# A mixture-of-experts block on one core: wider gathers of an expert's rows, and a search cut in three parts

## The reference

```python
g_prob = softmax(x @ w_rg + b_rg)            # 4 groups, the best one is taken
e_in_group = take_along_axis(e_logits, g_idx)  # 8 experts in it
e_top, e_idx = top_k(softmax(e_in_group), 2)   # the best two
expert = g_idx * 8 + e_idx                     # of 32 experts
...
def expert_block(args):
    xs, e = args
    gate, up = split(xs @ w_e_in[e], 2)        # 1024 x 1024 float32
    return (silu(gate) * up) @ w_e_out[e]      # 512 x 1024 float32
...
y = zeros((NT, D)).at[slot_tok].add(yb * slot_w[:, None])
x = x + gt2 * y
```

## Time and profile before

| | us |
|---|---|
| median of three runs | 1807.15 (1803.92 to 1807.35) |
| the profiled execution | 1807.53 |
| its span | 1805.7 |
| PE busy | 1682.9 (93% of the span) |
| DVE busy | 1014.3 (56%) |
| ACT busy | 442.2 (24%) |
| POOL busy | 235.0 (13%) |
| bytes moved | 334.20 MB, mean 185 GB/s |

### The profile page before, as it was taken

How to read it: one execution, slowest core, us unless ns; L and a number is a source line. 1 busy time by engine, 2 the same in 40 slices (tenths; PEclk the granted TensorE clock), 3 DMA queues, 4 the chain that set the end, 5 groups by cost and what they waited for, 6 DMA issues and landing times.

```text
span 1805.7 us, 35644 instructions
## 1 busy us (share of the span) xinstructions
PE 1682.9 (93%) x14825; PEld 932.5 (52%) x14825; DVE 1014.3 (56%) x2446; ACT 442.2 (24%) x1072; POOL 235.0 (13%) x359
## 2 busy tenths in 40 slices
PE   5999999999999999999999999969999998989890
PEld 3455444544445554555545545546777555555550
DVE  2486526564565345444444435556777777676754
ACT  5121323334443222222212311012222121212110
POOL 3030000000111122220222230010000000000003
PEclk9999999999999999999999999979999999999995
DMA  9377200001112011010110472368999999999997
GB/s 345 118 265 247 67 24 24 24 24 47 47 47 79 19 33 33 16 33 19 33 33 15 177 288 101 129 207 321 378 399 400 393 396 386 396 392 395 390 367 297
DMA packets 105413, 334.20 MB, mean 185 GB/s; under 512 B 13594, under 2 KB 57544, under 8 KB 93036
## 3 DMA queue, kind: packets, MB, share of 16 engines
q1 hardware_dynamic: 86256, 282.70, 42.2%
q0 software_dynamic: 8240, 25.04, 4.1%
q10 hardware_dynamic: 10828, 25.24, 3.9%
HBM read 299.51 MB, written 37.63 MB: 187 GB/s over the span
## 4 chain that ended last, share of the span: by engine, by line
PE 79%; DMA 14%; DVE 3%; issue 1%; POOL 1%; ACT 1%; SPq 1%; ACTq 0%; POOLq 0%; DVEq 0%
PE bank L296 77%; DMA arena<-in_w_e_in 10%; DMA arena<-in_w_e_out 2%; DMA arena<-in_w_in 1%; POOL arena L768 1%; PE bank L954 1%; DMA arena<-y_slots,ints 1%; SPq L378 1%; DVE arena L2390 0%; DVE arena L1884 0%; PE bank L1242 0%; DMA arena<-in_kn_g_c 0%; ACTq L1416 0%; DVE arena L2380 0%; DMA arena<-xnorm,ints 0%
## 5 line engine op out<-in xcount | busy, mean ns | idle before, releaser
L296 PE MATMUL bank<-arena 128*32 128x256 f32 (+9 forms) x14446 | 1641.0, 390 | 54.8 <-DMA arena<-in_w_e_in 21.7
L296 PEld LDWEIGHTS bank<-arena 128*32 128x32 f32 (+3 forms) x14446 | 887.3, 132 | 777.8 <-issue 562.4
L2380 DVE STREAM_TRANSPOSE arena<-arena 32x256 f32<-32x256 f32 x372 | 161.9, 435 | 5.7
L2390 DVE STREAM_TRANSPOSE arena<-arena 32x128 f32<-32x128 f32 x384 | 157.7, 411 | 4.8
L1734 ACT ACTIVATE arena<-bank 128x128 f32<-128x128 f32 x96 | 19.7, 278 | 420.9 <-PE bank L296 420.9
L2371 DVE TENSOR_TENSOR arena<-bank,arena 128x512 f32<-128x512 f32 x64 | 35.5, 558 | 103.3 <-PE bank L296 103.3
L1726 ACT ACTIVATE arena<-arena 128x96 f32<-128x96 f32 x248 | 92.1, 461 | 5.2 <-DVE arena L2380 5.2
L730 POOL DMA_INDIRECT arena<-xnorm,ints x32 | 31.4, 981 | 464.8 <-DVE arena L2380 446.7
L2141 DVE TENSOR_TENSOR arena<-arena,bank 128x128 f32<-128x128 f32 (+1 forms) x40 | 11.4, 286 | 130.3 <-PE bank L296 130.3
L681 POOL TENSOR_TENSOR arena<-arena 64x256 f32<-64x256 f32 x96 | 70.2, 731 | 30.3 <-DVE arena L2117 23.7
L1884 DVE RECIPROCAL arena<-arena 128x512 f32<-128x512 f32 x10 | 33.5, 3348 | 31.9 <-ACT arena L1471 31.9
(11 more groups left out here) (339 smaller groups left out, 1037.5 us busy)
## 6 DMA issues: line engine op xcount, KB each, us to landing
arena<-in_w_e_in SPq DMA_DIRECT2D x64, 2048.0 KB, 27.0
arena<-in_w_e_out SPq DMA_DIRECT2D x32, 2048.0 KB, 27.4
arena<-in_w_ada SPq DMA_DIRECT2D x12, 2048.0 KB, 12.9
arena<-in_w_in SPq DMA_DIRECT2D x32, 512.0 KB, 4.0
y_slots<-arena ACTq DMA_DIRECT2D x32, 288.0 KB, 9.4
y_slots<-arena POOLq DMA_DIRECT2D x21, 384.0 KB, 17.8
arena<-in_w_in SPq DMA_DIRECT2D x3, 2048.0 KB, 21.7
arena<-in_x SPq DMA_DIRECT2D x4, 1024.0 KB, 8.5
```

The lines of the kernel that those rows point to most:

```text
L296: return nc.tensor.matmul(o, l, r, start=start, stop=stop)
L2380: ins = V.transpose(e_xT[s][ts(b, QT), :, ts(t, QT)], rows[:, :, b, :])
L2390: ins = V.transpose(hT[ts(q, QT), :, ts(t, QT)], e_h[ts(c, QT), r, :].rearrange("p (n k) -> p k n", k=4))
```

## The change

There are two edits. The first: the gather of an expert's rows writes all 128 partitions of `e_xs[s]` and names the 128 indices of the column, where it wrote and named the first 96. The gathers of extra blocks, further on, still name 96. What DVE turns are the first 96 rows, as before. The second: `blocks_known` becomes three functions with the same instructions in the same order, and the loop over pairs from 2 to 7 and from 8 to 14 becomes four loops: pairs 2 to 4, 5 to 7, 8 to 10 and 11 to 14, with one function between each two.

```diff
--- before.py
+++ after.py
@@ -727,8 +727,8 @@
                     pool.wait_ge(sem("ix_set"), e - 1)
                     pool.wait_ge(sem("xs_used"), e - 1)
                 pool.sem_inc(sem("gather_go"), 1)
-                pool.indirect_dma_start(out=e_xs[s][0:CAP], out_offset=None, in_=xn_d,
-                                        in_offset=bass.IndirectOffsetOnAxis(ap=(i_ix[s] if wait else i_tab[:, e:e + 1])[0:CAP], axis=0),
+                pool.indirect_dma_start(out=e_xs[s], out_offset=None, in_=xn_d,
+                                        in_offset=bass.IndirectOffsetOnAxis(ap=i_ix[s] if wait else i_tab[:, e:e + 1], axis=0),
                                         bounds_check=T - 1, oob_is_err=False)\
                     .then_inc(sem(f"xs{s}_in"), 16)
             gather(0, 0, False)
@@ -2307,7 +2307,7 @@
             link(TT(r_w2, r_w1, r_te, ALU.mult))
             w1, w2 = r_w1, r_w2
 
-            def blocks_known():
+            def blocks_counted():
 
                 dve.wait_ge(sem("router_dve"), COUNTS)
                 link(TS(r_nx, r_cnt, float(CAP), None, ALU.is_gt))
@@ -2321,6 +2321,8 @@
                 link(TT(x_m, r_m, r_ov.unsqueeze(1).unsqueeze(1).to_broadcast([P, NT, TOPK, NE]), ALU.mult))
                 link(V.tensor_reduce(out=r_over, in_=x_m, axis=AX, op=ALU.add))
                 link(TS(r_own, r_v, -1.0, float(NE), ALU.mult, ALU.add))
+
+            def blocks_placed():
 
                 link(TS(r_div, r_rank, float(CAP), None, ALU.is_ge))
                 link(TT(r_over, r_over, r_div, ALU.mult))
@@ -2332,6 +2334,9 @@
                 link(STT(r_div, r_own, float(CAP), r_rank, ALU.mult, ALU.add))
                 for a, isl in enumerate((i_s1, i_s2)):
                     V.tensor_copy(isl, r_div[:, :, a])
+
+            def blocks_owned():
+
                 for j in range(NX):
                     ins = TS(r_ex[:, j, :], r_cum, float(j), None, ALU.is_le)
                 link(ins)
@@ -2423,10 +2428,16 @@
                 turn_h(e + 1)
                 turn_x(e + 3, 1, i + 1, e + 2)
 
-            with dve.Fori(2, NE // 4) as i:
+            with dve.Fori(2, 5) as i:
                 pair(i)
-            blocks_known()
-            with dve.Fori(NE // 4, NE // 2 - 1) as i:
+            blocks_counted()
+            with dve.Fori(5, 8) as i:
+                pair(i)
+            blocks_placed()
+            with dve.Fori(8, 11) as i:
+                pair(i)
+            blocks_owned()
+            with dve.Fori(11, NE // 2 - 1) as i:
                 pair(i)
             activate(NE - 2)
             y_out(NE - 3, 1, 32 * (NE // 2 - 2))
```

## The result

The changed kernel takes 1786.65 us (median of five runs, 1784.89 to 1787.55), the kernel before in the same job 1806.48 us. The ratio is 0.9892, with an interval of 0.9877 to 0.9906: 20 us faster. The forecast was 1818 us and the range began at 1795, so both missed, and the sign was the other one.

The account below looks back on a forecast made before the run. The prediction took PE, then from the later expert stage the DMA engines, to bound the kernel. Search 0, gathers +10.3 and first gather +0.4 made +10.7 us on 1807.53: 1818 us, range 1795 to 1829, its own range 1812 to 1829.

Parts of the forecast that it names:

- What bounds the kernel: Expert stage: PE sets the pace in the first window, later the DMA engines do, by 2.4 us an expert.
- The search: Search split in three, expert stage: PE's 5.34 us wait goes but is worth 0, bounds -0.6 us and 0.
- each part is shorter than that, and the wait goes: Search parts of 4.9, 3.3 and 3.4 us: each under the 6.3 us covered before, so PE's wait vanishes.
- The gathers: 24 gathers from 1290 to 1700 us: real rows crowd onto 8 engines, 0.43 us each, +10.3 us, bounds 8 and 21.
- +0.33 us for two rows more: Each gather: the fullest engine goes from six to eight rows at 0.167 us a row.
- +0.53 us for a longer dip: Under each gather: the dip from 432 to 331 GB/s lasts 9.1 us instead of 6.8, at the same depth.
- the dip goes: Rival, gathers: eight rows aligned with the weights' partitions end the dip, about 1779 us; faster by dip or stall, chance 0.26.
- half of that dip goes: Rival, gathers: -0.8 + 0.33 us each, so -11 us, 1796 us; within the 0.26 for faster.
- The first gather: Start of the expert stage, where PE waits 5.50 us for this gather alone: +0.4 us.
- What was to show it: Profile after: 9264 software packets, no PE wait near 1490, more weight waits, longer dips of the same depth.
- the 3.7 us by which the gathers were to land later: Each gather's landing, median 11.1 us, grows by 8/6; hidden, as its buffer is read two experts after issue.
- the bound of 29 us from PE's waits: Most that the vanished dip could gain: PE's 24.0 us of waits for weights plus 5.3 us behind DVE.

Follow-up runs that it names:

- e2: The changed kernel with gathers of 96 partitions again, so only the search in three parts differs from the kernel before: 1808.84 us, ratio 1.001.
- e1: The changed kernel with the search back in one piece, so only the gathers of 128 differ from the kernel before: 1783.91 us, ratio 0.9882.
- e4: The changed kernel with gathers of 112 partitions instead of 128: 1806.51 us, ratio 1.0002 to the kernel before.
- e6: e3 (ranks turned, search in three parts) with gathers of 96 partitions instead of 128: 1801.12 us, ratio 0.9973 to the kernel before.
- e3: The changed kernel with ranks turned: 0 to 31 at partitions 64 to 95, 32 to 63 at 0 to 31, 64 to 95 at 32 to 63: 1772.97 us.
- e8: e3 plus 29 plain loads of 384 KB on ACT's hardware queue, each writing 96 partitions of 4 KB, never read: 1840.12 us, ratio 1.0188.
- e9: e3 plus 29 plain loads of 384 KB on ACT's hardware queue, each writing 128 partitions of 3 KB, never read: 1799.64 us, ratio 0.9966.
- e5: The kernel before with every gather index past the bound, so 96 packets a gather move no row and experts work on zeros: 1772.34 us, ratio 0.9799.

## Why the prediction was wrong, point by point

**What bounds the kernel: right.** The DMA engines did set the pace after 1395 us, through a dip under each gather. All the gain came there.

**The search: right.** Its term was 0 with bounds of -0.6 and 0. e2 measures 1.001 (0.9999 to 1.002) against before, and the sum of PE's waits does not change. The wait did go, as the timeline after shows for the first part:

```profile
1388.20 0.17 DVE L2323 TENSOR_SCALAR arena<-arena 128x16 f32<-128x16 f32 x1
...
1388.67 0.68 DVE L2367 TENSOR_TENSOR arena<-arena,bank 128x128 f32<-128x128 f32 x3 [0.29 <-DVE arena L2323]
...
1389.50 10.78 PE L296 MATMUL bank<-arena 128*32 128x256 f32 x196 [1.43 <-DVE arena L2367]
```

Only this part leaves a rest, 1.4 us, against the step that "each part is shorter than that, and the wait goes": of 4.9 us of search 3.5 were covered. The 6.3 us that the prediction took as cover held only while PE itself was late for want of weights. In e1, where it was not, the search of 11.6 us stalls PE for 7.9, so 3.7 us are covered.

**The gathers: the failing step.** "A load counts as landed when its last engine is done, so the fullest engine sets the time": from it came +0.33 us for two rows more and +0.53 us for a longer dip, of which the sum took the middle, 24 x 0.43 = +10.3 us. The step that failed is the second of these: it kept the dip at its depth of 101 GB/s and asked only how long it would last. The runs show that it stands or falls with the shape of the write: there with 96 and 112 partitions, gone with 128 (e4 and the changed kernel), also in the turned order (e6 against e3), also for a plain load on the hardware queue (e8 against e9), and gone when the packets carry nothing (e5). The weight packets say the same. These are the 11794 packets of 16 KB that each trace holds after 1100 us, nearly all of those of the 96 loads:

| kernel | writes beside them | mean, ns | over 700 ns |
|---|---|---|---|
| before | 96 | 666.5 | 23% |
| e4 | 112 | 663.2 | 22% |
| e6 | 96, turned | 659.6 | 23% |
| e8 | 128, turned, and 96 plain | 667.4 | 23% |
| changed | 128 | 636.8 | 5% |
| e3 | 128, turned | 624.7 | 3% |
| e9 | 128, turned, and 128 plain | 626.1 | 3% |

From before to the changed kernel the mean falls by 29.7 ns, which for 11794 packets on 16 engines is 21.9 us: the size of the gain, 20 us.

The first half, that crowding the real rows costs something, was right in direction, but not shown in the way that I had thought. The late fall of the changed kernel goes when the ranks are turned, so where the real rows lie does matter. From the changed kernel to e3 the time of an expert falls by 17.1 - 16.2 = 0.9 us. Yet the fall comes late: between 1395 and 1515 us only one weight packet of 2830 took over 700 ns, between 1539 and 1700 it was 231 of 3638. That looks like a lag of the fuller engines that builds up until the buffers no longer hide it. In e1, where the stall of 7.9 us lets them catch up, the fall comes 100 us later. This is an inference, and one thing does not fit it: the DMA share stays at 1.00 at 408 GB/s, so the less loaded engines are not seen idle; their packets get longer. Nor can the fullest engine be the account of e6: with six rows an engine in blocks, the turn leaves six on the fullest, and still it gave 5 to 8 us.

For the change itself this means two terms of opposite sign. From e6 to e3 an expert falls from 17.5 to 16.2 us, 1.3 us, near the 1.6 us that the prediction had worked out for one dip; the fullest engine may have fewer real rows there too, so not all of it need be the shape. In the change only 0.8 of them are seen (17.9 to 17.1), since the real rows are crowded now. That is how the 20 us come out between the rivals "the dip goes" (-29) and "half of that dip goes" (-11). The mechanism was that of the first, to which I had given too little.

Why engines and partitions must agree is an inference: no row shows which engine writes which partition. The Trainium skill states it for 128 partitions (DMA: Bandwidth & Descriptors, "The descriptor swizzle"): each engine's eight descriptors go to partitions behind one port of the on-chip array. By that rule every weight load keeps each engine to its own port, and if a write of six or seven rows an engine is dealt in order, it can't; the traces agree as far as they reach, with 423 to 431 GB/s in the flights of 128 shown above and 331 in one of 96. By the same rule an engine's eight partitions are two groups of four, 32 apart, and not eight in a row: partitions 0 to 31 belong to engines 0 to 7, four each, and 64 to 95 to engines 8 to 15, four each. Of the two readings of "blocks" only this one lets the turn of e3 take the fullest engine from eight real rows to four, which at 427 / 16 = 26.7 GB/s would be 0.6 us of the 0.9; with eight partitions in a row, the plain reading, it would have left eight on the fullest, and the late fall should have stayed.

Two things remain open. That the loss is two engines meeting at one port was not tried. And no run tells the place of the rows from their number: a write of 96 partitions in which each engine keeps to the partitions of its weight loads would show whether six rows an engine do harm by themselves.

**A reading that was to be had from the profile before.** A gather's 64 rows of 4 KB are 0.26 MB, 0.6 us of all engines at 432 GB/s. A dip of 101 GB/s for 6.8 us loses 0.69 MB. A transfer that costs the others 2.6 times its own bytes disturbs them, and every term that counts its rows or packets misses that. I had both numbers and did not divide them.

**The first gather: small, as forecast, but not measured.** It was forecast at +0.4 us; from issue to PE's start it took 4.41 us against 4.25, +0.2 us. The same stretch was 4.60 us in e2, with 96 partitions, and 4.65 us in e1, with 128, so single executions differ by more than that.

**What was to show it.** 9264 packets: yes. No wait near 1490: yes. More waits for weights in its place: no, 13.3 us against 24.0, since the dip went. "Less than 17.9 us an expert would refute the gather's term": it was 17.1. The dips were to get longer at the same depth; they went. The landing median, 11.2 us, would have passed the step as right; it was no good sign, and the 3.7 us by which the gathers were to land later did not come.

**Slips in the sums.** -1.6 + 0.33 is -1.27 us, not -1.2, so 24 gathers are -30 us; the bound of 29 us from PE's waits holds all the same. The lower end of the forecast's own range, 1812 us, comes from no bound: 8 us give 1815. Neither changes the direction of the forecast.

The best version is e3, 1772.97 us (1771.16 to 1775.57): gathers of 128, ranks turned, search in three parts.

## What to carry to other kernels

Beside weight loads that fill the DMA engines, let even a small load into SBUF cover all 128 partitions: 96 cost some 1.3 to 1.4 us more each here (e6 against e3, e8 against e9), and the partitions beyond the data may be empty packets. This is shown for writes into SBUF alone. The output rows leave it from 96 partitions, and the changed kernel moves 423 GB/s from 1452.50 to 1459.00 right behind such a store, issued at 1452.51. Where skipped indices leave part of the partitions without data, place the real rows so that both halves of the partitions, 0 to 63 and 64 to 127, get their share. And compare what a dip loses with the bytes of the transfer beneath it: if it loses much more, ask how the transfer is written, not how long it is.

## What the runs showed of the hardware

- The core moved 426 to 428 GB/s over slices of 44 us (e3), with 96-partition writes in between 392 (before, 1539 to 1700). The gathers that made this difference are 0.26 MB of some 6.9 MB an expert. Their two causes don't add up simply: 128 partitions first give 408 GB/s and the turned ranks then 427; the turned ranks first give 399 (e6) and 128 partitions then 427.
- The loss lies in the duration of packets: beside a gather of 96 partitions 103 of 123 weight packets of 16 KB took over 700 ns, with none beside them 611 ns was the mean (before). That is more than the two thirds of the engines which by my assumption hold the real rows, so engines without such a row are likely slowed as well.
- A skipped index of an indirect DMA is a packet but moved nothing and slowed nothing that can be seen: 8240 packets with 8.38 MB less (e5), and 1024 packets more for no bytes (the changed kernel).
- A seventh row for each engine (112 partitions) was no better than the sixth: 389 GB/s against 392. With the eighth, and with it the same shape as a weight load, the dip was gone.
